# Moving the row bookkeeping of the last expert task forward, and gating its rows in other places

## The reference

```python
logits = (h @ w_router[i]).astype(F32)
top_v, top_i = lax.top_k(logits, TOP_K)            # 2 of 8 experts
top_w = jax.nn.softmax(top_v, axis=-1)
...
y = y + gates[..., e:e + 1] * swiglu(h, w_ex_gate[i, e], w_ex_up[i, e], w_ex_down[i, e])
...
xp = xp + g2 * channel_mixer(h2, ...)              # prompt: g2 from c_ctx; sample: g2 from c
y_prompt = rmsnorm(xp, final_g)                    # y_sample likewise
```

## Time and profile before

| | |
|---|---|
| median of 3 runs | 1532.15 us (1530.58 to 1533.17) |
| profiled execution | 1533.48 us, its span 1531.4 us |
| granted TensorE clock, mean | 0.989 |
| TensorE busy | 1484.0 us, 97% of the span |
| VectorE busy | 937.7 us, 61% |
| ScalarE busy | 786.7 us, 51% |
| GpSimd busy | 53.6 us, 4% |

### The profile page before, as it was taken

The page is one execution under the profiler, slowest core; times in us unless marked ns, Lnnn a source line. Parts: engine busy times, 40 slices in busy tenths (PEclk is TensorE's granted clock), DMA queues, the critical chain, the costliest instruction groups (busy, mean ns, idle before and its releaser), DMA issues.

```text
span 1531.4 us, 22089 instructions
## 1 busy us (share of the span) xinstructions
PE 1484.0 (97%) x8652; PEld 1308.3 (85%) x8652; DVE 937.7 (61%) x1077; ACT 786.7 (51%) x896; POOL 53.6 (4%) x54
## 2 busy tenths in 40 slices
PE   5999999999999999999999999998999999999997
PEld 4788969799899999997889696998888888888875
DVE  3542265555554254346522755556798898988988
ACT  4434354453432242235333544435778778787875
POOL 0100000000000000001000000000000000000002
PEclk8999999999999999999999999999999999999999
DMA  9754365467753544265333554535899999999994
GB/s 329 245 179 152 110 221 165 157 205 244 261 154 96 150 130 126 90 220 169 121 116 111 165 165 138 165 121 186 298 376 389 376 374 374 381 386 376 376 378 165
DMA packets 236026, 342.33 MB, mean 224 GB/s; under 512 B 8629, under 2 KB 156766, under 8 KB 235694
## 3 DMA queue, kind: packets, MB, share of 16 engines
q1 hardware_dynamic: 227392, 313.32, 59.9%
q0 software_dynamic: 6496, 24.69, 4.4%
q10 hardware_dynamic: 2062, 3.24, 0.6%
HBM read 325.74 MB, written 15.47 MB: 223 GB/s over the span
## 4 chain that ended last, share of the span: by engine, by line
PE 89%; DVE 5%; ACT 3%; DMA 1%; issue 1%; ACTq 0%; DVEq 0%; SPq 0%
PE ps L689 26%; PE ps L691 25%; PE ps L690 25%; PE ps L706 2%; DVE wlo L2142 2%; PE ps L887 1%; PE ps L921 1%; PE ps L905 1%; ACT whi L1575 1%; PE ps L1119 1%; PE ps L748 1%; ACT ebuf L1483 1%; PE ps L785 1%; PE ps L716 1%; DMA raw<-in_w_ada_dram 0%
## 5 line engine op out<-in xcount | busy, mean ns | idle before, releaser
L689 PE MATMUL ps<-hhi,whi 128*128 128x384 f32 x824 | 276.6, 336 | 0.3 <-DVE hidlo L2239 0.3
L691 PE MATMUL ps<-hhi,wlo 128*128 128x384 f32 x824 | 275.3, 334 | 0.0
L690 PE MATMUL ps<-hlo,whi 128*128 128x384 f32 x824 | 275.3, 334 | 0.0
L1763 DVE TENSOR_TENSOR wlo<-raw,whi 128x2048 fp32r<-128x2048 f32 x66 | 151.0, 2289 | 179.9 <-ACT whi L1317 168.3
L2142 DVE TENSOR_TENSOR wlo<-raw,whi 128x2048 fp32r<-128x2048 f32 (+1 forms) x81 | 179.0, 2227 | 27.4 <-ACT whi L1575 26.9
L1575 ACT ACTIVATE whi<-raw 128x2048 fp32r<-128x2048 f32 (+1 forms) x81 | 150.5, 1868 | 49.4 <-PE ps L691 47.8
L2142 DVE TENSOR_TENSOR wlo<-mraw,whi 128x2048 fp32r<-128x2048 f32 (+2 forms) x81 | 160.7, 1992 | 18.1 <-ACT whi L1575 17.6
L689 PE MATMUL ps<-whi,xgh 128*128 128x512 f32 (+1 forms) x432 | 164.7, 381 | 6.2 <-DVE wlo L2142 3.7
L1575 ACT ACTIVATE whi<-mraw 128x2048 fp32r<-128x2048 f32 (+2 forms) x81 | 136.6, 1686 | 53.2 <-PE ps L691 52.9
L691 PE MATMUL ps<-whi,xgl 128*128 128x512 f32 (+1 forms) x432 | 161.4, 374 | 0.0
L690 PE MATMUL ps<-wlo,xgh 128*128 128x512 f32 (+1 forms) x432 | 161.3, 373 | 0.0
(11 more groups left out here) (343 smaller groups left out, 2498.2 us busy)
## 6 DMA issues: line engine op xcount, KB each, us to landing
raw<-in_w_ada_dram SPq DMA_DIRECT2D x64, 512.0 KB, 5.4
raw<-in_w_ex_up_dram SPq DMA_DIRECT2D x27, 1024.0 KB, 6.7
raw<-in_w_ex_down_dram SPq DMA_DIRECT2D x27, 1024.0 KB, 5.1
raw<-in_w_gate_dram SPq DMA_DIRECT2D x48, 512.0 KB, 4.6
raw<-in_w_in_dram SPq DMA_DIRECT2D x44, 512.0 KB, 5.9
raw<-in_w_ex_gate_dram SPq DMA_DIRECT2D x18, 1024.0 KB, 7.3
mraw<-in_w_ex_gate_dram SPq DMA_DIRECT2D x18, 1024.0 KB, 7.8
mraw<-in_w_ex_down_dram SPq DMA_DIRECT2D x18, 1024.0 KB, 8.6
```

What stands on the lines that cost most here:

```text
L689: pe.matmul(out, s[0], m[0], start=first, stop=False, **kw)
L690: pe.matmul(out, s[0], m[1], start=False, stop=False, **kw)
L691: return pe.matmul(out, s[1], m[0], start=False, stop=last, **kw)
L1763: dve.tensor_tensor(wlo[:, n % RING, :], raw[:, n % RING, :], whi[:, n % RING, :].bitcast(F32), ALU.subtract).then_inc(lo_done, 1)
```

## The change

The three steps of bookkeeping move to slots 1, 2 and 3. The scaling of `ymin` moves on ScalarE to slots 11, 12 and 13, in the order of blocks 0, 1, 2; the sum with `ymax` moves on VectorE to slots 11, 13 and 15, one block each. GpSimd gates the prompt block's other rows and adds them to the residual, in two instructions; VectorE does the same for the two sample blocks, ahead of its wait for the last product. The down projection is gated as it leaves PSUM, by VectorE alone and twice (with the sample's gate row to `ysb`, with the prompt's to the new tile `yprompt`). TensorE then only picks the chosen rows, blocks in the order 1, 2, 0; VectorE adds them to what is ready, one instruction a block. The blocks are normed and written in that order as well.

```diff
+LAST = (1, 2, 0)
...
+            pool.wait_ge(rows_in, 48)
+            pool.wait_ge(others_sum, 1)
+            pool.tensor_tensor(ymax[:, 0, :], ymax[:, 0, :], rows[:, 1, :], ALU.mult).then_inc(prompt_sum, 1)
+            pool.wait_ge(prompt_sum, 1)
+            pool.tensor_tensor(ymax[:, 0, :], ymax[:, 0, :], xtok2[:, 0, :], ALU.add).then_inc(prompt_sum, 1)
...
             def last_rows(q):
-                def others(b, bank):
-                    for m in range(2):
-                        pe.matmul(ps[:, bank + m, :], ident, ymax[:, b, 512 * m:512 * m + 512], start=True, stop=False)
...
-                pe.wait_ge(others_sum, 1)
-                others(1, 2)
                 pe.wait_ge(choice_ready, 1)
-                pe.wait_ge(ya_ev, q + 2)
-                pe.wait_ge(yv_ev, q + 2)
-                chosen(0, 0, True)
-                chosen(1, 2, False)
-                pe.wait_ge(others_sum, 2)
-                others(2, 6)
-                chosen(2, 6, False)
+                for n, b in enumerate(LAST):
+                    for m in range(2):
+                        if b != 2:
+                            pe.wait_ge(y_gated, m + (1 if b else 3))
+                        y = ysb if b else yprompt
+                        mm = pe.matmul(ps[:, (0, 2, 6)[b] + m, :], gat[:, b, :], y[:, 512 * m:512 * m + 512], start=True, stop=True)
+                    mm.then_inc(rows_mm, 1)
...
+                    if s in (11, 12, 13) and not more:
+                        b = s - 11
                         act.wait_ge(row_ready, 1)
-                        for b in (1, 2, 0):
+                        act.wait_ge(ymin_in[b], 16)
+                        act.activation(ymin[:, b, :], ymin[:, b, :], ACT.Identity, scale=wrow[:, 0, b:b + 1]
+                                       ).then_inc(ymin_scaled, 1)
...
-                    if s == 3 and not more:
+                    if s == 1 and not more:
                         shares()
-                    if s == 5 and not more:
+                    if s == 2 and not more:
                         row_numbers()
-                    if s == 7 and not more:
+                    if s == 3 and not more:
                         row_shares()
                     if s == 9 and not more:
                         choice(q)
-                    if s == E_UNIT - 3 and not more:
-                        for n, b in enumerate((1, 2, 0)):
+                    if s in (11, 13, 15) and not more:
+                        b = (s - 11) // 2
+                        dve.wait_ge(ymax_in[b], 16)
+                        dve.wait_ge(ymin_scaled, b + 1)
+                        dve.scalar_tensor_tensor(ymax[:, b, :], ymax[:, b, :], wrow[:, 2, b:b + 1], ymin[:, b, :], ALU.mult,
+                                                 ALU.add).then_inc(others_sum, 1)
...
+                if not more:
+                    dve.wait_ge(rows_in, 48)
+                    for b in (1, 2):
+                        dve.wait_ge(others_sum, b + 1)
+                        link(dve.tensor_tensor(ymax[:, b, :], ymax[:, b, :], rows[:, 0, :], ALU.mult))
+                        link(dve.tensor_tensor(ymax[:, b, :], ymax[:, b, :], xtok2[:, b, :], ALU.add))
                 dve.wait_ge(mm_done, q * E_UNIT + (n0 + E_UNIT))
                 dve.wait_ge(yd_out, q * 16 + 32)
+                if not more:
+                    for v in range(2):
+                        for m in range(2):
+                            c = slice(512 * m, 512 * m + 512)
+                            dve.tensor_tensor((ysb, yprompt)[v][:, c], ps[:, 4 + m, :], rows[:, v, c], ALU.mult).then_inc(y_gated, 1)
+                    return
...
-                link(gated(0, ymax[:, 0, :]))
-                for b in range(BLK):
-                    from_rows(b)
-                    if b:
-                        scaled(b - 1)
+                for n in range(BLK):
+                    from_rows(n)
+                    if n:
+                        scaled(n - 1)
                 scaled(BLK - 1)
```

More of the change, by code:

```diff
@@ L253, in prefix_step_kernel @@
         evalu = at("evalu", 512, oraw_at + 2048)
+        yprompt = at("yprompt", D, oraw_at)
         gat = at("gat", T, oraw_at + 4096, shape=[BLK, P])
@@ L1169, in last_rows @@
             def last_rows(q):
-                def others(b, bank):
+                pe.wait_ge(choice_ready, 1)
+                for n, b in enumerate(LAST):
                     for m in range(2):
-                        pe.matmul(ps[:, bank + m, :], ident, ymax[:, b, 512 * m:512 * m + 512], start=True, stop=False)
-                def chosen(b, bank, first):
-                    for m in range(2):
-                        mm = pe.matmul(ps[:, bank + m, :], gat[:, b, :], ysb[:, 512 * m:512 * m + 512], start=first, stop=True)
+                        if b != 2:
+                            pe.wait_ge(y_gated, m + (1 if b else 3))
+                        y = ysb if b else yprompt
+                        mm = pe.matmul(ps[:, (0, 2, 6)[b] + m, :], gat[:, b, :], y[:, 512 * m:512 * m + 512], start=True, stop=True)
                     mm.then_inc(rows_mm, 1)
-                pe.wait_ge(others_sum, 1)
-                others(1, 2)
-                pe.wait_ge(choice_ready, 1)
-                pe.wait_ge(ya_ev, q + 2)
-                pe.wait_ge(yv_ev, q + 2)
-                chosen(0, 0, True)
-                chosen(1, 2, False)
-                pe.wait_ge(others_sum, 2)
-                others(2, 6)
-                chosen(2, 6, False)
             def experts():
@@ L1629, in experts @@
                 act.activation(fin[:, 1, 0:1], epsc[:, :], ACT.Sqrt)
-                for b in range(BLK):
-                    act.wait_ge(fin_x, b + 1)
+                for n, b in enumerate(LAST):
+                    act.wait_ge(fin_x, n + 1)
                     act.activation(ysq[:, :], xtok2[:, b, :], ACT.Square, accum_out=fin[:, 0, b:b + 1]).then_inc(fin_sq, 1)
-                    act.wait_ge(fin_sq, b + 1)
+                    act.wait_ge(fin_sq, n + 1)
                     act.activation(fin[:, 1, b:b + 1], fin[:, 0, b:b + 1], ACT.Sqrt, scale=1.0 / D, bias=epsc[:, 0:1]
@@ L2167, in expert_task @@
                         token_of(q + 2, 1)
+                    if s == 1 and not more:
+                        shares()
+                    if s == 2 and not more:
+                        row_numbers()
                     if s == 3 and not more:
-                        shares()
-                    if s == 5 and not more:
-                        row_numbers()
-                    if s == 7 and not more:
                         row_shares()
@@ L2193, in experts, with from_rows, scaled @@
                 expert_task(last, False)
[L2195 to L2200, removed]
-                    bank = (0, 2, 6)[b]
-                    gated(b, ps[:, bank:bank + 2, :].rearrange("p a c -> p (a c)")).then_inc(fin_x, 1)
-                def scaled(b):
-                    dve.wait_ge(fin_std, b + 1)
+                def from_rows(n):
+                    b = LAST[n]
+                    dve.wait_ge(rows_mm, n + 1)
+                    if b == 0:
+                        dve.wait_ge(prompt_sum, 2)
+                    bank = (0, 2, 6)[b]
+                    dve.tensor_tensor(xtok2[:, b, :], ymax[:, b, :], ps[:, bank:bank + 2, :].rearrange("p a c -> p (a c)"), ALU.add
+                                      ).then_inc(fin_x, 1)
+                def scaled(n):
+                    b = LAST[n]
+                    dve.wait_ge(fin_std, n + 1)
                     link(dve.reciprocal(fin[:, 1, b:b + 1], fin[:, 1, b:b + 1]))
@@ L2208, in scaled @@
                                              ALU.mult, ALU.mult).then_inc(fin_y, 1)
-                dve.wait_ge(rows_in, 48)
-                dve.wait_ge(others_sum, 3)
-                link(gated(0, ymax[:, 0, :]))
-                for b in range(BLK):
-                    from_rows(b)
-                    if b:
-                        scaled(b - 1)
+                for n in range(BLK):
+                    from_rows(n)
+                    if n:
+                        scaled(n - 1)
                 scaled(BLK - 1)
```

9 lines of the change are left out of this document (3 added, 6 removed).

## The result

The kernel after takes 1539.45 us (median of 11 runs, 1535.14 to 1544.34), the kernel before 1532.31 (median of 11). The ratio is 1.0042, with a 95% interval of 1.0029 to 1.0055: slower by about 6.4 us, 4.4 to 8.4 by that interval (the medians differ by 7.1). The profiled execution of after is the one of 1539.45 us, its span 1537.7.

The account below looks back on a forecast made before the run. VectorE's list of work was taken to decide nearly the whole end. +0.6 us for parts 1 to 4 and +1.9 for GpSimd's hold made +2.5: a median of 1534.7 us, range 1530.8 to 1537.8.

Parts of the forecast that it names:

- VectorE's longer list and the bookkeeping: Last task: bookkeeping costs +0.1 to +0.3 us, VectorE's list grows 0.7; the end comes 0.6 us later.
- Part 4: The tail from VectorE's PSUM gating to its last end: 11.35 us, with 1.72 us a product pair on TensorE.
- Part 3: Two sample blocks gated ahead on VectorE: 5.0 us, of which 3.1 lie behind the last product.
- Part 5: GpSimd's two instructions: 1.5 us each; if VectorE waits for them, a hold of 1.9 us before the PSUM gating.
- the rival of the full hold: GpSimd holds VectorE for its full length, 2.7 us an instruction: +4.9, 1537.1 us; chance 0.32.
- The collision with the weights: Rival: gathers 10 us earlier delay down pieces, piece 14 landing near 1499.7; VectorE idles up to 2 us; chance 0.10.
- The bookkeeping's own cost: Bookkeeping moved to slots 1 to 3: +0.1 to +0.3 us by slot 12.
- The gathers' start: With the cast at 1479.5, the first gather issues at 1480.6 and not 1490.17.
- VectorE's 0.7 us more work: VectorE's list with the gating ahead and the new tail: 11.15 us in place of 10.4.
- That the gating ahead would not be hidden: Against the rival that it is hidden (-3.9 us, 1528.3, chance 0.08): VectorE has 1.1 us idle, 5.0 are wanted.
- the walk itself: VectorE's instructions followed in order through the last task: it reaches the PSUM gating at 1517.5 without a hold.
- One sign: In the changed profile, the PSUM gating starts about 3 us behind the last product, 5 with a hold.

Follow-up runs that it names:

- filler products: The kernel after, with four float32 products added on TensorE between the last product and the picking of rows: 66.13 us for the stretch, ratio 1.0029.
- without GpSimd's work, beside the fillers: The kernel after, without GpSimd's two instructions and with four added products in TensorE's pause: 63.83 us for the stretch, ratio 1.0012.
- all three repaired: The kernel after, with the cast in slot 7, sums in slot 15, GpSimd beside PSUM reads, four added TensorE products: stretch 62.20 us, ratio 0.9997.
- the residual on TensorE: The repaired kernel, with bookkeeping back in slots 3, 5, 7 and the added products made identity by sample blocks' residual: stretch 61.12 us, ratio 1.0003.

## Why the prediction was wrong

The forecast was 1534.7 us and no measurable change, the range 1530.8 to 1537.8; the median is 1539.45. The stretch accounts for it: 7.54 us more, of which +2.5 was forecast. Taking one cost out after the other gives 69.04, 66.13, 63.83, 62.20 and 61.50 (single traces; the ratios of the whole times move with them):

| term | forecast | measured | from |
|---|---|---|---|
| TensorE's clock in the tail | 0 | 2.9 | filler products |
| GpSimd holds VectorE | 1.9 | 2.3 | without GpSimd's work, beside the fillers |
| weights late behind the gathers, with the sums and scalings moved back in the same step | 0 (a rival of 0.10) | 1.6 | that kernel against all three repaired |
| VectorE's longer list and the bookkeeping | 0.6 | 0.7 | all three repaired |

The sizes depend on the order: the hold alone, taken out first, was worth 3.1, and the early gathers alone, put into the kernel before, cost 2.0.

**Part 4, the step that failed.** "A product pair took 3.60/2 less overlap, 1.72" was carried over from a TensorE that had been busy up to that moment. Part 3 had itself worked out that TensorE would stand idle for 3.1 us before the gating, and drew nothing from it. The idle engine came back at half its clock, and the products were on the path, since VectorE waits for each block. The tail was 14.17 us and not 11.35; with the clock kept up it was 11.32. The Trainium skill, page TensorE: Matmul & The Clock Gate, section "What's actually happening", says that an idle TensorE is put to half rate, 1.2 GHz. The trace agrees in the kernel after: granted clock 0.50 behind a pause of 3.80 us, 1.00 behind pauses of 0.38, 1.05 and 1.76. In the kernel without GpSimd's work the clock was still 1.00 at the end of a pause of 3.83 us and fell 0.7 us after TensorE was at work again; why it fell later there stays open. In the trace of before the same row was at hand: the earlier trace rows show a mean clock of 0.82 in the last stretch, where it cost nothing, since no product followed.

**Part 5, right in kind, small in size.** The direction that no row had shown is there: `wlo` 14 stood until GpSimd's multiply was done. The Trainium skill, page SBUF — State Buffer, section "SBUF: two separate sides", says that the loser is blocked fully; the trace agrees, by the 2.15 us from the end of the multiply to the end of `wlo` 14. An instruction took 2.39 and not 1.5 us, which is over the 1.8 from which the rival of the full hold (chance 0.32) was to decide; so on this term that rival came true. The estimate of 2.4 us by the Trainium skill, page GPSIMD Engine Reference, section "Performance versus the Vector engine", agrees with the trace. The place was off too: GpSimd got in between two back-to-back instructions of VectorE (`wlo` 14 and 15), where I had let it wait for a read of PSUM, as the gather of 4.56 us had done. The sum of the two stretches was 3.15 us, 2.3 after what the late weights would have cost at the same place.

**The collision with the weights** was held to be a rival with a chance of 0.10 and a price of 2.0. It happened, in the form described there: piece 14 landed at about 1500.7 on the clock of before, a microsecond behind the 1499.7 given there, and the price was 2.0 us alone, about 1.6 here. It didn't exclude the other cases, as a list of rivals with one chance each makes it look; hold and late weights come together, and their sum alone passes the forecast.

**The other steps held.** The bookkeeping's own cost: 0.26 us. The gathers' start: 1480.3 against 1480.6. VectorE's 0.7 us more work: 0.8. That the gating ahead would not be hidden: it ran from 1515.32 to 1520.31, TensorE idle beside it. VectorE's arrival at the PSUM gating, 1521.7 on the clock of before, is 1517.5 plus 3.15 of hold plus 1.01 of waiting for piece 14: the walk itself came out within 0.1 us, its inputs did not. One sign was misread in advance: a hold was to put the gating 5 us behind the last product in place of 3. It was 3.0, since the same late `wlo` held up TensorE too, whose last product ended at 1518.7 on the clock of before and not at 1515.3.

The 7.54 us of the stretch lie inside the interval of the whole times, 4.4 to 8.4. Whether anything outside the stretch changed stays open: the start of the last task differs from run to run (1463.9 to 1468.1 in these traces), for reasons ahead of the change.

## What to carry to other kernels

Where a step moves work ahead of a wait, ask what each other engine does in the time that it now stands still: TensorE's pause of 3.8 cost this kernel 2.9 us, and four useless products bought it back. Two instructions of GpSimd of 2.4 us each cost nothing beside VectorE's reads of PSUM and held it for 3.15 to 4.3 us beside two-operand reads of SBUF, so their place matters more than their number. Gathers that started 10 us sooner than needed took their bandwidth from weights that were just in time.

## What the runs showed of the hardware

- Pauses of TensorE of nearly the same length had different prices: behind 3.80 us (the kernel after) the eight records took 6.53 us, behind 3.83 (without GpSimd's work) and 3.81 (its work beside the reads of PSUM) 5.37, and 3.60 at full clock. In the first the clock fell 1.0 us before the picking began, in the other two 0.7 and 1.0 us after.
- GpSimd and a VectorE instruction with two operands in SBUF block each other in turns, at the grain of one instruction: a `wlo` of 4.49 us is 2.21 longer than the 2.28 that it takes alone. The wait shows as duration, not as idle time; a reader who looks for gaps alone doesn't see it.
- A float32 multiply or add of 128x1024 took 2.35 to 2.39 us on GpSimd, beside 1.22 on VectorE.
- A gather's issue did not get in between two back-to-back `wlo` as GpSimd's add did: it sat through both (4.56 us in the kernel before, 4.57 with the residual on TensorE) and ended 0.8 us behind the second.
